# The first norm's transposes: from TensorE to DMA transposes on SP's queue, for three of five groups

## The chip, the cores and the metric

The kernel runs on the 8 cores of one Trainium2 chip, with no communication between them. Cores 0 to 3 take four consecutive quarters (2048 tokens each) of the first sequence, cores 4 to 7 those of the second. The metric is the device time in microseconds of the slowest core.

## The reference

One layer of a diffusion backbone: token mixing (windowed attention with context keys, and a gated spatial MLP per chunk of 128 tokens), then a SwiGLU FFN, each behind a layer norm whose result is scaled and shifted. Cut to the part around the change:

```python
def modulate(y, shift, scale):
    return y * (1 + scale[..., None, :]) + shift[..., None, :]

mod_x = jnp.split(jax.nn.silu(c) @ w_ada[layer] + b_ada[layer], 6, axis=-1)
hc = modulate(layer_norm(ctx), mod_c[0], mod_c[1])     # context tokens
kc, vc = context_kv(hc, w_in[layer])
h = modulate(layer_norm(x), mod_x[0], mod_x[1])        # latent tokens, D_MODEL = 1024
mix = token_mixer(h, *mix_params, kc, vc, (rows, cols))
x_mid = post_norm(x, mod_x[2][:, None, :] * mix, ln1_g[layer], ln1_b[layer])
```

token_mixer multiplies h by w_in: q and k (with rotary positions), v, the two halves u and vb of the gated branch, and two gates.

## The kernel before

The matmuls want the normalised tokens with the 1024 features on the partitions: hT is a bf16 tile of 128 partitions x 8 chunks x 2304 tokens (hcT the same for 256 context tokens). The tokens come in five groups of four 128-token tiles. Groups 0 to 3 are the core's own 2048 tokens; group 4, the outer group, is the tile before, the tile after and the two context tiles. In words of the change's title, group 2 is the third, group 3 the fourth and group 4 the outer one.

For each group:

- x_load (line 289) brings a tile of 128 tokens x 1024 f32, 512 KB, into xin[i], issued from SP.
- ln_stats (lines 413 to 415, VectorE, called DVE in the profile), ln_rstd (lines 418 to 422, GpSimd, called POOL, and DVE).
- ln_norm (line 428, ScalarE, called ACT) writes the normalised tile xnh[i] in bf16 and then has SP issue the x load of the next group into the same xin[i].
- ln_turn (line 442) transposes 128x128 blocks on TensorE (PE) into PSUM banks, a pair of chunks at a time: 8 transposes for 4 tiles.
- ln_out (lines 459 and 463) takes a chunk from PSUM to hT, multiplies by 1 + scale and adds the shift, both per partition (modc, by mcol). Chunks 0, 1, 4 and 5 go by ACT (line 459), 2, 3, 6 and 7 by DVE (line 463).

The projections of a group are units of eight matmuls each: qk_mm (line 488, with the rotary part in qk_rope: one matmul, line 499, two DVE products, lines 503 and 505, one POOL sum, line 511), u_unit (line 528), vb_unit (line 558, followed by a norm of its own in vn_stats and vn_norm, lines 570 to 581) and v_unit (line 540). One do() call emits the units of one group in a written order, and side work behind unit n is taken from a dictionary: side_of(g, at, last) builds it for the norm of the next group. During the units of group g - 1 the positions are: statistics at at + i, norm at at + 4 + i (for the outer group at + i), transposes and evictions from at + 8 on (at + 4 for the outer group). Group 2 has at = 1, groups 3 and 4 have at = 0, and positions over `last` (12; 7 for the outer group) are moved to it.

Other side work in the same stretch: p0_issue loads a block of w_ada (1 MB as bf16, issued from POOL) into one of two buffers, p0_compute multiplies it (lines 349 or 394) and DVE adds the bias (lines 359 or 399). rope_load brings the cosine and sine tables. Each engine runs its queue in the order in which it was emitted. The class Sched puts semaphore waits in front of an instruction for what it depends on.

A transpose by DMA is issued from one queue only, SP's.

Of the kernel before, what the change touches and what calls it, by code (L numbers as in the profile page):

```python
# [9 lines left out]
ALU = mybir.AluOpType  # L10
# [129 lines left out]
def build_nc(debug_stop=None):  # L140
    nc = bass.Bass("TRN2", target_bir_lowering=False)
    es = ExitStack()
    S = Sched()
# [68 lines left out]
    hT, _, nbA = A.alloc(BF16, [8, TH])  # L212
# [36 lines left out]
    def colpos(ti):  # L249
        return {0: 2048, NT + 1: 2176}.get(ti, (ti - 1) * 128)  # L250
# [6 lines left out]
    hcT, _, nb = A.alloc(BF16, [8, CTX], at=o); o += nb  # L257
# [13 lines left out]
    xnh = [A.alloc(BF16, [D], at=at)[0] for at in (  # L271
        RD + 16 * 1024, RD + 18 * 1024, RE_FREE + 20 * 1024, RE_FREE + 22 * 1024)]
# [5 lines left out]
    groups = [[('x', 1 + 4 * g + i) for i in range(4)] for g in range(4)]  # L278
# [46 lines left out]
    def sp_consts():  # L325
        t_gb.append(sp_load(g1bc, badabc_d[:, 0:1024], 'g1b'))
        t_gb.append(sp_load(g2bc, badabc_d[:, 1024:2048], 'g2b'))
        for dst, src in ((bsbc, bsbc_d), (esink, esink_d), (glgc, glgc_d)):
# [7 lines left out]
                 deps=[t_sc])  # L336
# [29 lines left out]
    def mcol(kind, chunk, which):  # L366
        return modc4[:, kind, chunk, which:which + 1]
# [37 lines left out]
    ln = [dict(ag=[None] * 4, xn=[None] * 4) for _ in groups]  # L405
    xnh_free = [None] * 4
    mv_free = [None] * 4
    t_hT = [[None] * 8 for _ in groups]
# [57 lines left out]
            fb_free[banks[n // 2]] = t_hT[g][c] = t_e  # L466


    qraw_free = [None, None]
    rt_free = [None, None]  # L470
    t_qg = [[] for _ in range(4)]
# [123 lines left out]
    t_mod = [[], []]  # L595
# [5 lines left out]
        t_mod[blk % 2].append(t_e)  # L601
    ln_out(0, list(range(8)), [4, 5, 6, 7], t_mod)

    PAIRS = [((0, 1), (3,)), ((2, 3), (6,)), ((4, 5), (7,)), ((6, 7), (3,))]

    def group_seq(g):
        s = []
        if g == 0:
            for n, (kd, m) in enumerate(first):
                s += [(u_unit, m, g)] if kd == 'u' else [(qk_mm, m, g)]  # L610
                if n and first[n - 1][0] == 'q':
                    s += [(qk_rope,)]
            s += [(vb_unit, g, 0), (qk_rope,), (vb_unit, g, 1), (vb_unit, g, 2), (vb_unit, g, 3)]
        else:
            for m in range(4):
                s += [(qk_mm, m, g), (u_unit, m, g), (qk_rope,), (vb_unit, g, m)]
            s += [(qk_mm, 4, g)]
        return s
# [23 lines left out]
    def side_of(g, at, last):  # L642
        side = {}

        def put(n, *work):
            side.setdefault(min(n, last), []).extend(work)

        for i in range(4):
            if g < 4:
                put(at + i, (ln_stats, g, i))  # L650
                put(at + 4 + i, (ln_norm, g, i))
            else:
                put(at + i, (ln_norm, g, i))
            n = at + (8 if g < 4 else 4) + i
            if i:
                put(n, (ln_out, g) + PAIRS[i - 1] + (t_mod,))
            put(n, (ln_turn, g) + PAIRS[i])
        if g < 4:
            side[at + 3].append((ln_rstd, g))
        put(n + 1, (ln_out, g) + PAIRS[3] + (t_mod,))  # L660
        return side

    def bs_sum():
# [8 lines left out]
    def add(side, n, *work):  # L672
        side.setdefault(n, []).extend(work)

    s1 = side_of(2, 1, 12)
    add(s1, 1, (sp_consts,))
    add(s1, 2, (p0_issue,))
    add(s1, 3, (cb_load,))
    add(s1, 6, (p0_compute, 6))
    add(s1, 12, (p0_issue,))  # L680
    s2 = side_of(3, 0, 12)
    add(s2, 1, (p0_compute, 7), (p0_issue,))
    add(s2, 3, (bs_sum,))
# [12 lines left out]


    s3 = side_of(4, 0, 7)
    add(s3, 1, (p0_compute, 1), (p0_issue,))
    add(s3, 7, (p0_compute, 0), (p0_compute, 1))  # L700
# [3 lines left out]
    for k in range(8):  # L704
        t_mm = S.op('pe', lambda e, k=k, pq=bk(b_)[:, 0:CTX]: e.matmul(pq, lhsT=wqk[:, 4, k, :], rhs=hcT[:, k, :],
                                                                     start=(k == 0), stop=(k == 7)),
                    deps=[fb_free[b_], t_hT[4]] if k == 0 else (), sig=(k == 7))
# [420 lines left out]
    for t in range(NT):  # L1128
# [7 lines left out]
        if t % 4 == 3:  # L1136
            g = t // 4
# [21 lines left out]
    for n, (r, tg) in enumerate(order):  # L1159
# [14 lines left out]
        if tg == 3:  # L1174
            if r + NWR < NR:
                load_w1(r + NWR)
            if r == 2:
                for i in range(2, NR):
# [4 lines left out]
                    out=scb2, in_=sc[:, 0:8].unsqueeze(2).to_broadcast([128, 8, 128])), deps=[t_wg2])  # L1183
# [239 lines left out]
```

How the kernel before makes its waits and increments, by code:

```python
            def body(engine, items=items):  # L93
                for (ws, fn, sigkey, inc) in items:
                    for (p, t) in ws:
                        engine.wait_ge(sems[p], t)
                    if fn is None:
                        continue
                    ins = fn(engine)
                    if sigkey is not None:
                        ins.then_inc(sems[sigkey], inc)
```

## Time and profile before

| | |
|---|---|
| median of 3 runs | 987.92 us (987.78 to 989.19) |
| the profiled execution | 987.81 us |
| its span on the slowest core (core 6) | 986.3 us |
| spans of the 8 cores | 978.2 to 986.3 us |
| PE busy | 901.2 us, 91% of the span |
| DVE, ACT, POOL busy | 471.0, 297.2, 243.4 us |
| DMA packets | 41069, 95.50 MB |

The stretch of the trace that the change touches runs from about 84 to 182 us: the units of groups 1, 2, 3 and 4. Times in the rows are microseconds from the start of the span unless marked ns. In a timeline a row is: start, time taken by the row's instructions together, engine, line, operation, and what was idle before it with what ended the wait. A busy PE row ends later than its successor begins, because matmuls are pipelined.

### The profile page before, as it was taken

What the parts mean: (1) busy time and instruction counts of PE and PEld (TensorE: products, weight loads), DVE (VectorE), ACT (ScalarE), POOL (GpSimd) and SP (SyncE); (2) the same over time, 40 slices, a digit from 0 to 9 for tenths busy, and PEclk for the clock granted to TensorE, in tenths of its full rate; (3) what the DMA queues carried; (4) which work ended last, traced back from release to release, by engine and by line L of the source; (5) the groups of instructions that cost most, each with busy time, mean ns of one, the idle gap of its engine ahead of it and who ended that gap; (6) DMA issues with size and microseconds to landing.
All of it is one profiled execution on the core that took longest, in us unless ns stands there. A gap on an engine that the chain in (4) does not pass through costs nothing.

```text
span 986.3 us, 15419 instructions; the slowest of 8 cores (978.2 to 986.3 us)
## 1 busy us (share of the span) xinstructions
PE 901.2 (91%) x5401; PEld 434.9 (44%) x5401; DVE 471.0 (48%) x930; ACT 297.2 (30%) x408; POOL 243.4 (25%) x282
## 2 busy tenths in 40 slices
PE   0569998899999999999989999999999999999993
PEld 0324444445444444444444444444444444444443
DVE  2146665376632456656666321121122114777775
ACT  1215555599922232433333311111111111000000
POOL 5023333256532345555543003010000000000000
PEclk9989999999999999999999999999999999999997
DMA  9988876069720022217713039972211004233231
GB/s 169 169 190 204 175 177 95 3 118 178 137 108 1 1 87 85 73 57 164 157 65 86 22 53 158 167 114 43 35 16 36 1 1 150 92 122 113 101 107 45
DMA packets 41069, 95.50 MB, mean 97 GB/s; under 512 B 4000, under 2 KB 4512, under 8 KB 40992
## 3 DMA queue, kind: packets, MB, share of 16 engines
q0 software_dynamic: 21136, 40.44, 26.6%
q1 hardware_dynamic: 19856, 54.06, 16.9%
q8 instruction: 45, 0.74, 0.3%
q14 instruction: 32, 0.26, 0.1%
HBM read 118.14 MB, written 16.78 MB: 137 GB/s over the span
## 4 chain that ended last, share of the span: by engine, by line
PE 77%; DMA 9%; ACT 5%; DVE 3%; issue 3%; POOL 1%; another core or an unknown queue 0%; SPq 0%; DVEq 0%; ACTq 0%; POOLq 0%
PE bank L1088 30%; PE bank L953 16%; PE bank L1223 14%; DMA arena<-wada 7%; PE bank L984 5%; ACT arena L812 3%; PE bank L488 2%; DMA arena<-xh 2%; PE bank L809 1%; PE bank L558 1%; PE bank L805 1%; PE bank L528 1%; PE bank L828 1%; ACT arena L428 1%; PE bank L1041 1%
## 5 line engine op out<-in xcount | busy, mean ns | idle before, releaser
L1088 PE MATMUL bank<-arena 128*128 128x512 bf16 x1408 | 305.4, 379 | 0.0
L1088 PEld LDWEIGHTS bank<-arena 128*128 128x128 bf16 x1408 | 137.6, 98 | 165.4
L953 PE MATMUL bank<-arena 128*128 128x512 bf16 x768 | 168.0, 379 | 0.0
L1099 DVE TENSOR_TENSOR arena<-bank,arena 128x512 bf16<-128x512 f32 x88 | 60.9, 692 | 224.2 <-PE bank L1088 217.2
L1223 PE MATMUL bank<-arena 128*128 128x512 bf16 (+1 forms) x748 | 152.2, 366 | 0.0
L1097 ACT ACTIVATE arena<-bank 128x512 f32<-128x512 f32 x88 | 52.4, 595 | 224.9 <-PE bank L1088 224.9
L953 PEld LDWEIGHTS bank<-arena 128*128 128x128 bf16 x768 | 75.0, 98 | 89.9
L1223 PEld LDWEIGHTS bank<-arena 128*128 128x128 bf16 x748 | 73.2, 98 | 79.1
L969 DVE TENSOR_TENSOR arena<-bank,arena 128x512 f32<-128x512 f32 x64 | 44.3, 692 | 94.0 <-PE bank L953 94.0
L812 ACT ACTIVATE arena<-bank 128x1024 bf16<-128x1024 f32 x80 | 76.3, 1027 | 4.8 <-PE bank L809 4.5
L962 ACT ACTIVATE arena<-bank 128x512 f32<-128x512 f32 x64 | 37.0, 591 | 118.9 <-PE bank L953 118.9
L971 POOL TENSOR_TENSOR arena<-arena 128x512 bf16<-128x512 f32 x32 | 50.4, 1575 | 71.1 <-DVE arena L969 48.7
L984 PE MATMUL bank<-arena 128*128 128x512 bf16 x256 | 59.0, 384 | 0.0
L1017 ACT ACTIVATE arena<-arena 128x1024 f32<-128x1024 f32 (+1 forms) x32 | 38.5, 1235 | 45.0 <-DVE arena L1015 45.0
L243 POOL DMA_DIRECT2D arena<-wff x22 | 16.4, 763 | 132.9 <-PE bank L1088 132.9
L511 POOL TENSOR_TENSOR arena<-arena 128x512 bf16<-128x512 f32 (+1 forms) x21 | 26.1, 1242 | 86.7 <-DVE arena L505 86.7
L488 PE MATMUL bank<-arena 128*128 128x512 bf16 (+1 forms) x168 | 39.8, 380 | 6.7 <-DMA arena<-wqk 2.6
L1244 ACT ACTIVATE arena<-arena 128x1 f32<-128x1 f32 x16 | 4.7, 294 | 136.3 <-DVE arena L1243 136.3
L1024 POOL TENSOR_TENSOR arena<-arena 128x1024 f32<-128x1024 f32 x16 | 37.7, 2355 | 18.6 <-ACT arena L1017 18.4
L984 PEld LDWEIGHTS bank<-arena 128*128 128x128 bf16 x256 | 25.3, 99 | 30.3 <-issue 1.4
L809 PE MATMUL bank<-arena 64*128 64x512 bf16 x160 | 31.3, 384 | 6.4 <-ACT arena L812 2.7
L558 PE MATMUL bank<-arena 128*128 128x512 bf16 x128 | 33.4, 410 | 3.1 <-DMA arena<-wvvb 3.1
(110 smaller groups left out, 867.2 us busy)
## 6 DMA issues: line engine op xcount, KB each, us to landing
arena<-xh SPq DMA_DIRECT2D x34, 512.0 KB, 6.9
arena<-wada POOLq DMA_DIRECT2D x12, 1024.0 KB, 16.9
arena<-wff POOLq DMA_DIRECT2D x11, 1024.0 KB, 10.4
xmid_d<-arena SPq DMA_DIRECT2D x16, 512.0 KB, 2.9
arena<-xmid_d SPq DMA_DIRECT2D x16, 512.0 KB, 3.7
out<-arena SPq DMA_DIRECT2D x32, 256.0 KB, 2.0
arena<-wff POOLq DMA_DIRECT2D x11, 512.0 KB, 20.6
arena<-wout SPq DMA_DIRECT2D x16, 256.0 KB, 5.4
```

The source lines that it names most:

```text
L488: t_mm = S.op('pe', lambda e, k=k, pq=pq, m=m, rhs=hT[:, k, g * 512:g * 512 + n_]: e.matmul(pq, lhsT=wqk[:, m, k, :], rhs=rhs, start=(k == ...
L558: t_mm = S.op('pe', lambda e, k=k, pvb=bk(b_), lh=hT[:, k, mt * 128:(mt + 1) * 128]: e.matmul(pvb, lhsT=lh, rhs=wvvb[:, k, 128:640], start ...
L809: t_mm = S.op('pe', lambda e, psb=bk(2 * i2 + kv), ksrc=ksrc, kv=kv, j=j, first=not masked: e.matmul(psb, lhsT=ksrc[kv * 64:(kv + 1) * 64, ...
L812: t_e = S.op('act', lambda e, pt=PT[slot], psb=bk2(2 * i2): e.activation(out=pt.rearrange('p a b -> p (a b)'), in_=psb, func=AF.Exp, scale ...
L953: t_mm = S.op('pe', lambda e, k=k, n=n, p=bk(bank), lhs=w[:, lo + k, :], rhs=src[:, k, tok]: e.matmul(p, lhsT=lhs, rhs=rhs, start=(k == 0) ...
L969: fb_free[2 + i] = t_p = S.op('dve', lambda e, dst=sga[r + i], p=bk(2 + i): e.tensor_tensor(out=dst, in0=p, in1=dst, op=ALU.mult), deps=[d ...
L971: t_merged[(m, tg)] = S.op('pool', lambda e, dst=merged[tg % 2][:, m, :], a=sga[r], b=sga[r + 1]: e.tensor_tensor(out=dst, in0=a, in1=b, o ...
L984: rhs=woutb[:, k, half * 512:(half + 1) * 512]: e.matmul(p, lhsT=lhs, rhs=rhs, start=(k == 0), stop=(k == 7)),
L1088: rhs=h2T[:, k, tok]: e.matmul(p, lhsT=lhs, rhs=rhs, start=(k == 0), stop=(k == 7)),
L1097: fb_free[b0] = t_s = S.op('act', lambda e, dst=sgb[s_], p=bk(b0): e.activation(out=dst, in_=p, func=AF.Silu), deps=[t_p[0], sg_free[s_]])
L1099: fb_free[b0 + 1] = sg_free[s_] = t_act[(f, tg)] = S.op('dve', lambda e, f=f, p=bk(b0 + 1), sg=sgb[s_]: e.tensor_tensor(out=act[f][:, tok] ...
L1223: t_mm = S.op('pe', lambda e, pd=bk(b_)[:, 0:cs.stop - cs.start], f=f, t=t, cs=cs: e.matmul(pd, lhsT=act[f][:, t * 128:(t + 1) * 128], rhs ...
```

## The change

For groups 2, 3 and 4 ln_turn and ln_out are replaced by ln_dturn and ln_dmod. ln_dturn(g, i) has SP issue one DMA transpose of a whole tile, xnh[i] (128 tokens x 1024) to the tile's columns in all 8 chunks of hT or hcT. Its completion also frees xnh[i] for the next group. ln_dmod(g, (c, c + 1)) scales and shifts these two chunks in place on DVE once all four transposes of the group are complete; in the outer group each chunk takes two instructions, one for the 256 latent tokens and one for the 256 context tokens. Groups 0 and 1 keep the transposes on PE. The transposes are put right behind the norm of their tile, the ln_dmods at the positions where the evictions stood.

```diff
+    def ln_dturn(g, i):
+        kindt, ti = groups[g][i]
+        dst = hT[:, :, colpos(ti):colpos(ti) + 128] if kindt == 'x' else hcT[:, :, ti * 128:(ti + 1) * 128]
+        xnh_free[i] = ln[g][('dt', i)] = S.dma('sp', lambda e, dst=dst, src=xnh[i]: e.dma_start_transpose(out=dst, in_=src),
+                                               'hturn%d' % i, deps=[ln[g]['xn'][i]])
+
+    def ln_dmod(g, chunks, t_mod):
+        for c in chunks:
+            for h, which in [(hT[:, c, g * 512:(g + 1) * 512], 0)] if g < 4 else [(hT[:, c, 2048:2304], 0), (hcT[:, c, :], 1)]:
+                t_hT[g][c] = S.op('dve', lambda e, h=h, c=c, which=which: e.tensor_scalar(
+                    out=h, in0=h, scalar1=mcol(1, c, which), scalar2=mcol(0, c, which), op0=ALU.mult, op1=ALU.add),
+                    deps=[[ln[g][('dt', i)] for i in range(4)], t_mod[c // 4]])
...
-    PAIRS = [((0, 1), (3,)), ((2, 3), (6,)), ((4, 5), (7,)), ((6, 7), (3,))]
-
...
                 put(at + i, (ln_norm, g, i))
-            n = at + (8 if g < 4 else 4) + i
-            if i:
-                put(n, (ln_out, g) + PAIRS[i - 1] + (t_mod,))
-            put(n, (ln_turn, g) + PAIRS[i])
+            put(at + (4 if g < 4 else 0) + i, (ln_dturn, g, i))
+            put(at + (9 if g < 4 else 5) + i, (ln_dmod, g, (2 * i, 2 * i + 1), t_mod))
         if g < 4:
             side[at + 3].append((ln_rstd, g))
-        put(n + 1, (ln_out, g) + PAIRS[3] + (t_mod,))
         return side
```

## Rows read from the trace of the kernel before

**Rows 1.** The page: busy time, and the chain that ended last.

```profile
PE 901.2 (91%) x5401; PEld 434.9 (44%) x5401; DVE 471.0 (48%) x930; ACT 297.2 (30%) x408; POOL 243.4 (25%) x282
...
PE 77%; DMA 9%; ACT 5%; DVE 3%; issue 3%; POOL 1%; another core or an unknown queue 0%; SPq 0%; DVEq 0%; ACTq 0%; POOLq 0%
```

**Rows 2.** Timeline of PE: the end of group 1's units.

```profile
116.23 0.61 PE L442 MATMUL bank<-arena 128*128 128x128 bf16 x8
116.67 1.95 PE L540 MATMUL bank<-arena 128*128 128x128 bf16 x32
...
118.68 1.89 PE L488 MATMUL bank<-arena 128*128 128x512 bf16 x8
```

**Rows 3.** The chain that ended last, 84 to 190 us: start, length, piece.

```profile
149.59 0.99 DVE arena L463 x2
...
159.40 14.89 DMA arena<-wada
```

**Rows 4.** Timeline of ACT: an eviction pair, the last norm.

```profile
112.42 1.44 ACT L459 ACTIVATE arena<-bank,arena 128x512 bf16<-128x512 bf16 x2
...
163.73 1.23 ACT L428 ACTIVATE arena<-arena 128x1024 bf16<-128x1024 f32 x1
```

**Rows 5.** Line 289 in three short windows: issue times, time to landing.

```profile
L289 SPq DMA_DIRECT2D arena<-xh x1: 328/328/328, 107.8 to 107.8; - x1
...
DMA to landing us min/median/max: 10.8/10.8/10.8
...
L289 SPq DMA_DIRECT2D arena<-xh x1: 327/327/327, 109.8 to 109.8; - x1
...
DMA to landing us min/median/max: 9.9/9.9/9.9
...
L289 SPq DMA_DIRECT2D arena<-ctxb x1: 328/328/328, 139.3 to 139.3; - x1
...
DMA to landing us min/median/max: 5.6/5.6/5.6
```

**Rows 6.** Timeline of DVE.

```profile
111.30 0.68 DVE L503 TENSOR_TENSOR arena<-bank,arena 128x512 f32<-128x512 f32 x1
...
115.39 0.69 DVE L570 BATCH_NORM_STATS2 arena<-arena 128x6 f32<-128x512 f32 x1 [2.10 <-ACT arena L562]
116.19 0.18 DVE L571 BATCH_NORM_AGGREGATE arena<-arena 128x2 f32<-128x6 f32 x1
...
117.58 0.55 DVE L581 TENSOR_SCALAR arena<-arena 128x512 bf16<-128x512 f32 x1 [0.33 <-POOL arena L574]
...
142.48 0.99 DVE L463 TENSOR_SCALAR arena<-bank,arena 128x512 bf16<-128x512 bf16 x2
```

**Rows 7.** Windows: busy us of each engine, granted clock, DMA share, GB/s.

```profile
112.00:116.00 4.00, 4.00 (x29) 2.13 (x27) 1.30 (x2) 2.46 (x4) 1.27 (x1) 1.00 0.98 287
116.00:120.00 4.00, 4.00 (x50) 3.04 (x49) 3.57 (x9) 2.53 (x4) 1.76 (x3) 1.00 0.16 55
...
140.00:144.00 4.00, 4.00 (x32) 2.29 (x31) 2.69 (x7) 2.28 (x4) 1.48 (x3) 1.00 0.91 324
```

**Rows 8.** DMA queues (packets, MB, share), 134.5:145 and then 155:175 us.

```profile
q1 hardware_dynamic: 576, 2.10, 62.2%
q0 software_dynamic: 130, 0.23, 12.2%
...
q0 software_dynamic: 1056, 2.10, 71.0%
q1 hardware_dynamic: 288, 0.26, 6.8%
```

**Rows 9.** Timeline of PE after its longest idle time of the stage.

```profile
156.99 0.99 PE L349 MATMUL bank<-arena 128*128 128x2 bf16 x32 [3.41 <-DVE arena L505]
157.84 2.54 PE L528 MATMUL bank<-arena 128*128 128x512 bf16 x8
160.17 2.97 PE L558 MATMUL bank<-arena 128*128 128x512 bf16 x8
```

## The prediction

> **What bounds it now.** I read the page first. TensorE (PE) is busy for 901.2 of 986.3 us and holds 77% of the chain that ended last, so a microsecond taken from its queue is a microsecond of the span unless something else ends last there [rows 1]. The change touches only the input stage, so I then read PE's timeline there, from 84 to 182 us. It is a string of units of eight matmuls, one every 1.73 us. The eight transposes of a pair of chunks sit between two units and push the next one back by 0.44 us, as from 116.23 to 116.67 [rows 2]. Next I followed the chain that ended last through the same stretch. It leaves PE for long pieces: at 149.59 us it is on the queue of VectorE (DVE), in the scale-and-shift of line 463, and at 159.40 us it is in a load of w_ada that takes 14.89 us; only when that has landed, at 174.3, do PE's matmuls go on [rows 3]. So near the end of this stage DVE's order and the DMA engines set the pace, and PE time saved there is worth nothing.
>
> **What is removed.** 96 transposes leave PE: 12 pairs at 0.44 us, 5.3 us in all. ACT loses its evictions of line 459, 1.44 us a pair of chunks [rows 4]. It waits for PE between most of its operations here, so I value that at nothing.
>
> **What is added to SP's queue, and what stands before it.** ln_norm(g, i) issues the x load of the next group, and ln_dturn(g, i) comes right behind it. SP's order is x(3,0), turn(2,0), x(3,1), turn(2,1) and so on to x(3,3), turn(2,3). A turn waits for the same norm as the load ahead of it, so SP waits no longer than now. But the last transpose is behind a load of 512 KB. In group 2 the last two loads go out at 107.8 and 109.8 us and take 10.8 and 9.9 us, so they land at 118.6 and 119.7, in the order of issue; in group 3 the last goes out at 139.3 and lands 5.6 us later, at 144.9 [rows 5]. If that order holds for transposes as well, the four turns of group 2 are complete no earlier than 119.7 us, however quick they are, and those of group 3 no earlier than 144.9.
>
> Who waits: every ln_dmod depends on all four transposes of its group, and DVE runs its queue in order. DVE meets the first ln_dmod of group 2 just before the rope product that starts at 111.3 us, and that of group 3 at 142.5 us, where a line-463 pair stands now [rows 6]. Behind it on DVE are the rope products, the statistics of the gated branch and the other ln_dmods; PE waits for all of these.
>
> **The price of a transpose** is not in this trace. Each moves 256 KB from SBUF to SBUF. Lower end: at the 324 GB/s seen from 140 to 144 us it costs 0.8 us of all 16 DMA engines [rows 7]. Upper end: each run of 128 columns of one token (256 bytes, 1,024 of them) costs what a small packet costs. From 155 to 175 us 288 packets of the hardware queue, 0.26 MB, took 6.8% of 16 engines for 20 us: 76 ns each, 1.36 us for the quarter megabyte [rows 8]. 1,024 such packets on 16 engines are 4.9 us. I take 2.0 us, near the 1.36 us row and above it, since the pieces are smaller than its packets. Four are 8.0 us per group (3.2 to 19.6).
>
> The Trainium skill, "DMA: Bandwidth & Descriptors", section "Latency and other measured facts", gives 261 GB/s for a DMA transpose with a non-contiguous middle dimension, by estimate 1.0 us each, and with it the sum below would be some 12 us smaller. The Trainium skill, "VectorE: DVE Perf Modes", section "The three transpose paths", speaks against the change: 1309 ns for 128x128 by DMA, 390 ns by TensorE, and TensorE is its advice where the result may go to PSUM. Eight such blocks one after another would by estimate be 10.5 us a transpose and over 100 us in the sum. No row here shows either.
>
> The engines don't stand idle for this. Their share is 0.98 from 112 to 116 us and 0.16 from 116 to 120 [rows 7]: some 2 us are free before 119.7 (part of the rest is the tail of a landing). From 134.5 to 145 us the two queues take 62.2 and 12.2%, so about 2.5 us are free. From 155 to 175 they take 71.0 and 6.8%, of which I give the transposes 2 us [rows 8]. So the landings move back by 6.0, 5.5 and 6.0 us (fast end 1.2, 0.7, 1.2; slow end 17.6, 17.1, 17.6).
>
> **ln_dmod** works on 128x512 bf16 in place in SBUF. Nearest rows: the line-581 normalisation of as many elements, 0.55 us, and the smallest DVE operation beside it, 0.18 us [rows 6]. I take 0.35. Eight are 2.8 us against four evictions at 0.48 (0.96 to 0.99 a pair): +0.9 us per group (-0.5 to +2.5).
>
> **Group 2, step by step.** T is the landing, 119.7 + 6.0 = 125.7. DVE then does two ln_dmods (0.7), two rope products (1.2), statistics and aggregate (0.9), two ln_dmods (0.7): T + 3.5. From the aggregate at 116.19 to the normalisation at 117.58 GpSimd has a step of its own, 1.3 us, so the next normalisation ends at T + 4.6, and the last four ln_dmods at T + 6.0. The first unit of the next group needs the last chunk and so ends at T + 6.2 = 131.9. Now it starts at 118.68 [rows 2] and ends at 120.4. Shift: 11.5 us. The PE time saved in this group lies inside the wait. PE is idle some 10 us in it, and after an idle time of 3.41 us the next two units take 2.54 and 2.97 us in place of 1.89 [rows 9]; I add 1.5 us for that, DVE's backlog hiding the rest.
>
> **Group 3.** In the old times the landing is at 144.9 + 5.5 = 150.4 against DVE's arrival at 142.5. DVE has little idle time from there to 156, and the chain runs through it. Shift: 7.9 + 0.9 = 8.8 us.
>
> **Outer group.** There are no x loads behind its norms, the last of which ends at 165.0 [rows 4]. Its transposes meet the w_ada loads. Its hT is wanted only after the landing at 174.3, so its own landing has 9 us of cover. But that w_ada load is what PE waits for: +6.0 us. The 1.8 us of PE time saved in front of it only lengthen the wait.
>
> Sum: 11.5 + 1.5 + 8.8 + 6.0 = 27.8 us, no PE saving counted. What follows (attention, then FFN) is mostly a closed chain of PE, so it moves as a whole. Against the profiled execution's own 987.8 us (span 986.3 and 1.5 around it; the median of the runs is 987.92, the same to 0.1): 1016 us. Fast end: 6.7 + 1.5 + 4.0 + 1.2 = 13.4, 1001 us. Slow end: 23.1 + 1.5 + 20.4 + 17.6 = 62.6, 1050 us.
>
> **Rivals.**
> (a) The transposes run at plain speed and only the order of the queue costs: 1001 us. For it: they are bytes on the same 16 engines. Against it: 256-byte pieces.
> (b) They are slow: a full packet's cost for each piece, or one after another at what the last 512 KB load took here, 5.6 us [rows 5]. That is the slow end and a little above, 1050 to 1058 us. If a piece costs two packets, one for its reading and one for its writing, it is 9.8 us a transpose, 94 us above my case: 1110 us. The second page of the skill cited above comes out near that.
> (c) The transposes are hidden and the kernel is faster. Mechanism: the order of the queue doesn't bind, so a turn overtakes the load ahead of it. The point is at DVE's arrival: complete by 112 us in group 2 and by 143 in group 3, DVE never waits, and the 8 pairs of these groups save 3.5 us of PE time: 984 us. Against it: that is some 2 and 4 us after the last issue, and the loads in front of them take 9.9 and 5.6.
> (d) Part of the waits remain and the PE time pays for them: no change.
>
> **How the numbers follow.** Chances: my case 0.46 (its own range 1004 to 1032), (a) 0.16, (b) 0.20 up to 1058 and 0.09 beyond, (c) 0.06, (d) 0.03. The likeliest gives 1016. From 996 to 1054 us leaves out (c), (d), the part of (b) near 1110 and a little of the rest. 0.2%, 2 us, is about what a measurement of this kernel can tell from no change: faster 0.06, within it 0.03, slower 0.91.
>
> **What would show it.** Right: 12 transposes on SP's queue; DVE's longest waits are at the new scale-and-shift line, released by a DMA, some 14 us in group 2 and 8 in group 3; PE idle before the first unit that reads hT of group 2 and before the first that reads hT of group 3; the last w_ada load of the stage takes some 20 us to land, not 14.89; from attention on the durations are as before. Wrong: if the turns land within 5 us of issue, the order of the queue was no bound; if a transpose takes more than 3 us of the engines, its price is off and the time is near 1050 us; if the wait in group 3 is absorbed, the chain was not DVE's there.

## The result, and the profile after

The change made the kernel slower. The ratio to the kernel before is 1.0333, with a 95% interval of 1.0296 to 1.0371: 32.9 us more (29 to 37), a time of about 1021 us. The forecast was 1016 us, or 28 us more, in a range from 996 to 1054. All ratios here and below are of executions in which no half of the chip ran at a lower granted clock than the other; of the changed kernel one execution of four (1093.65 us) is left out for that.

The profiled execution (1023.05 us, span 1021.5, slowest core 2) in parts 1, 3 and 4 of the page:

```profile
PE 899.5 (88%) x5228; PEld 431.2 (42%) x5305; DVE 475.4 (47%) x946; ACT 288.3 (28%) x392; POOL 242.8 (24%) x282
...
q0 software_dynamic: 21136, 40.44, 25.4%
q1 hardware_dynamic: 32528, 57.20, 19.5%
...
PE 72%; DMA 7%; DVE 5%; ACT 5%; SPq 4%; issue 4%; POOL 1%; another core or an unknown queue 0%; DVEq 0%; ACTq 0%; POOLq 0%
```

PE is as busy as before [rows 1] in a longer span (77 of its 5305 matmuls, going by the weight loads, are missing from the trace), and the chain that ended last now has 4% on SPq, that is on SP's own instructions. The hardware queue has 12,672 packets more, 1,056 for each of the 12 transposes; by their number and the bytes, that is the 1,024 pieces of 256 bytes and 32 small ones more.

SP's timeline through the input stage: start, time from there to the end of the row's last instruction, line (472 is the transpose, 289 the x load).

```profile
103.25 0.33 SPq L289 DMA_DIRECT2D arena<-xh  x1
103.63 3.20 SPq L472 DMA_TRANSPOSE arena<-arena  x1
106.94 0.51 SPq L289 DMA_DIRECT2D arena<-xh  x1
107.49 5.38 SPq L472 DMA_TRANSPOSE arena<-arena  x1
...
116.33 2.96 SPq L472 DMA_TRANSPOSE arena<-arena  x1
...
145.76 1.32 SPq L472 DMA_TRANSPOSE arena<-arena  x1
...
153.66 1.70 SPq L472 DMA_TRANSPOSE arena<-arena  x1
...
175.21 24.32 SPq L472 DMA_TRANSPOSE arena<-arena  x4
```

This is the part that I had left out. An x load holds SP for 0.33 to 0.53 us; a transpose holds it for 1.3 us at the least and for 5.4 in group 2, and in the outer group four take 24.3 us. In group 2 the second x load goes out 3.7 us behind the first, where it was 1.6 us before, and the next transposes slip with it.

DVE's timeline at the three landings; line 478 is the in-place scale and shift, and the bracket is the wait with what ended it.

```profile
122.70 0.74 DVE L478 TENSOR_SCALAR arena<-arena 128x512 bf16<-128x512 bf16 x2 [11.56 <-DMA arena<-arena]
...
158.99 1.38 DVE L478 TENSOR_SCALAR arena<-arena 128x512 bf16<-128x512 bf16 x4 [5.51 <-DMA arena<-arena]
...
203.36 1.11 DVE L478 TENSOR_SCALAR arena<-arena 128x256 bf16<-128x256 bf16 x4 [16.67 <-DMA arena<-arena]
```

Three waits, 11.6, 5.5 and 16.7 us. The two first were forecast at 14 and 8. The third was not forecast. PE's timeline shows how they arrive at PE:

```profile
124.89 0.58 PE L513 MATMUL bank<-arena 128*128 128x512 bf16 x1 [8.37 <-DVE arena L519]
...
129.85 3.35 PE L542 MATMUL bank<-arena 128*128 128x512 bf16 x8
133.03 1.89 PE L394 MATMUL bank<-arena 128*128 128x512 bf16 x8
...
163.67 2.77 PE L542 MATMUL bank<-arena 128*128 128x512 bf16 x6 [5.10 <-DVE arena L519]
...
174.37 0.99 PE L349 MATMUL bank<-arena 128*128 128x2 bf16 x32 [4.51 <-DVE arena L519]
...
199.14 0.99 PE L349 MATMUL bank<-arena 128*128 128x2 bf16 x32 [9.94 <-DMA arena<-wada]
204.11 0.89 PE L502 MATMUL bank<-arena 128*128 128x256 bf16 x2 [3.97 <-DVE arena L478]
...
216.61 0.39 PE L818 MATMUL bank<-arena 64*128 64x512 bf16 x2 [1.76 <-POOL arena L525]
```

The same instructions in the kernel before:

```profile
122.13 1.89 PE L394 MATMUL bank<-arena 128*128 128x512 bf16 x8
...
174.43 0.99 PE L349 MATMUL bank<-arena 128*128 128x2 bf16 x32 [1.70 <-DMA arena<-wada]
...
182.49 0.39 PE L809 MATMUL bank<-arena 64*128 64x512 bf16 x2 [1.75 <-POOL arena L511]
```

With them the loss can be split by place. The multiplication of a w_ada block that is line 394 in both kernels was at 122.13 us and is at 133.03: 10.9 us for group 2. That of line 349, at 156.99 [rows 9], is at 174.37: 17.4 in all, so 6.5 for group 3. The first score matmul of the attention was at 182.49 and is at 216.61: 34.1 in all, so 16.7 for the outer group. The outer group's part divides once more. The multiplication that waits for the last w_ada load was at 174.43 and is at 199.14, 24.7 us later, so 7.3 of the 16.7 us are the late w_ada load; the other 9.4 us come behind it, from the late transposes, DVE's backlog and the lower clock. From there to the end the shift grows by about 1 us more; the spans of the two profiled executions differ by 35.2.

### The profile page after: what moved, and what is told of

Read it like the earlier page. It is cut to its first block, busy times and chain, and to the rows that moved or that the text cites. A ratio compares the mean times of both kernels' runs of the same rounds, so it can differ in the third digit from the quotient of the medians.

```text
span 1021.5 us, 15196 instructions; the slowest of 8 cores (1011.9 to 1021.5 us)
## 1 busy us (share of the span) xinstructions
PE 899.5 (88%) x5228; PEld 431.2 (42%) x5305; DVE 475.4 (47%) x946; ACT 288.3 (28%) x392; POOL 242.8 (24%) x282
## 4 chain that ended last, share of the span: by engine, by line
PE 72%; DMA 7%; DVE 5%; ACT 5%; SPq 4%; issue 4%; POOL 1%; another core or an unknown queue 0%; DVEq 0%; ACTq 0%; POOLq 0%
PE bank L1097 29%; PE bank L962 16%; PE bank L1232 14%; PE bank L993 5%; SPq L472 4%; DMA arena<-wada 3%; ACT arena L821 3%; DMA arena<-xh 2%; DMA arena<-arena 2%; PE bank L818 1%; PE bank L502 1%; PE bank L837 1%; PE bank L814 1%; DVE arena L478 1%; PE bank L572 1%
## 5 line engine op out<-in xcount | busy, mean ns | idle before, releaser
L1232 PE MATMUL bank<-arena 128*128 128x512 bf16 (+1 forms) x735 | 151.5, 366 | 0.7
L502 PE MATMUL bank<-arena 128*128 128x512 bf16 (+1 forms) x163 | 43.0, 401 | 15.1 <-DVE arena L478 6.9
```

Of the source, the lines that this page charges most:

```text
L502: t_mm = S.op('pe', lambda e, k=k, pq=pq, m=m, rhs=hT[:, k, g * 512:g * 512 + n_]: e.matmul(pq, lhsT=wqk[:, m, k, :], rhs=rhs, start=(k == ...
L1232: t_mm = S.op('pe', lambda e, pd=bk(b_)[:, 0:cs.stop - cs.start], f=f, t=t, cs=cs: e.matmul(pd, lhsT=act[f][:, t * 128:(t + 1) * 128], rhs ...
```

## Experiments

The time differences below are ratio less 1, times 988 us. First, one group at a time.

### The outer group back on PE, and the outer group alone

Without its first line, which lists the chunk pairs of ln_turn again:

```diff
+    DMA_GROUPS = (2, 3)
...
+            if g in DMA_GROUPS:
                 put(at + (4 if g < 4 else 0) + i, (ln_dturn, g, i))
                 put(at + (9 if g < 4 else 5) + i, (ln_dmod, g, (2 * i, 2 * i + 1), t_mod))
+            else:
+                n = at + (8 if g < 4 else 4) + i
+                if i:
+                    put(n, (ln_out, g) + PAIRS[i - 1] + (t_mod,))
+                put(n, (ln_turn, g) + PAIRS[i])
...
+        if g not in DMA_GROUPS:
+            put(n + 1, (ln_out, g) + PAIRS[3] + (t_mod,))
```

In the second kernel DMA_GROUPS is (4,).

Expected of groups 2 and 3 by DMA:

> Groups 2 and 3 by DMA, the outer group back on PE. In the changed kernel's profile the PE units of the outer group's stage came 33 us later than before, of which 17 us were there already at its start. If each group's loss stands by itself, this kernel is 17 to 18 us slower than before: about 1005 us. Rival: the outer group's loss is a follow-up of the earlier shifts (w_ada loads issued later than before meet other traffic), so that they remain here in part: 1010 to 1018 us.

Measured: 1.0176 (1.0149 to 1.0203), 17.4 us.

Expected of the outer group alone by DMA:

> Only the outer group by DMA. If its loss stands by itself: 15 to 16 us slower than before, about 1003 to 1004 us, with the four transposes taking some 20 us of SP's time, as in the changed kernel, next to the two w_ada loads. Rival as for the kernel above: the loss needs the earlier shifts, and alone the outer group costs what I had predicted for it, 6 us: 994 us.

Measured: 1.0136 (1.0118 to 1.0154), 13.4 us. On core 0 the four transposes take 23.0 us of SP's time, about as expected; no other time is read from its trace. So the outer group's loss is its own, not a follow-up of the earlier shifts, and it is twice the 6 us of my prediction.

### Group 2 alone, group 3 alone

The same edit with DMA_GROUPS = (2,) and (3,). Expected of group 2 alone:

> Only group 2 by DMA, in the order of the change. Groups 2 and 3 together cost 17.4 us. If the parts add up, and from the shift of 10 to 11 us behind group 2 in the changed kernel's trace: 10 to 11 us slower than before, about 999 us. Rival: group 3's wait absorbs part of it when both are moved, so group 2 alone costs 12 us or more.

Measured: 1.0104 (1.0085 to 1.0123), 10.3 us. Expected of group 3 alone:

> Only group 3 by DMA, in the order of the change (each transpose behind an x load). With the transposes first it cost 3.6 us. Theory of the queue's order: the last transpose lands 4 to 6 us later for DVE, so 5 to 9 us slower than before, 994 to 997 us. Rival: the order matters only in company with the other groups, 991 to 992 us.

Measured: 1.0102 (1.0083 to 1.0121), 10.1 us, a microsecond over the upper end that I had given. DVE waits 6.72 us for the last transpose here. Groups 2 and 3 together cost 17.4, not 20.4. The wait of group 3 is shorter, 5.51 us, when DVE and PE have been set back by group 2, which may be the reason, but the intervals allow a plain sum too. One by one the three groups make 33.8 us, the whole change 32.9.

### The transposes ahead of the x loads

```diff
+    TURNS_FIRST = (2, 3, 4)
...
-        if g + 1 < len(groups):
+        if g + 1 < len(groups) and g not in TURNS_FIRST:
             x_load(g + 1, i, t_wada0[3])
...
+        if i == 3 and g + 1 < len(groups) and g in TURNS_FIRST:
+            for k in range(4):
+                x_load(g + 1, k, t_wada0[3])
```

The last three lines stand at the end of ln_dturn.

> All three groups by DMA; SP issues a group's four transposes before the four x loads of the next group, not in turn with them. Theory of the queue's order (the last transpose has to wait for the x loads in front of it): the last landing comes 4 to 6 us after the last norm of a group rather than some 13 us in group 2 and 9 in group 3; 4 to 6 us less in each of the two groups, about 1013 us. Rival: the order costs nothing, since SP and the engines move the same bytes either way and the x loads come late for the statistics instead: 1020 to 1025 us.

Measured: 1.0229 (1.0202 to 1.0255), 22.6 us, that is 10.3 us less than the change as made. SP's timeline and DVE's first ln_dmod of groups 2 and 3 (line 474 is the transpose here, 483 the ln_dmod):

```profile
101.39 10.06 SPq L474 DMA_TRANSPOSE arena<-arena  x4
111.50 2.00 SPq L289 DMA_DIRECT2D arena<-xh  x4
...
135.87 6.07 SPq L474 DMA_TRANSPOSE arena<-arena  x4
```

```profile
113.94 0.73 DVE L483 TENSOR_SCALAR arena<-arena 128x512 bf16<-128x512 bf16 x2 [4.91 <-DMA arena<-arena]
...
144.09 1.38 DVE L483 TENSOR_SCALAR arena<-arena 128x512 bf16<-128x512 bf16 x4
```

DVE's wait in group 2 falls from 11.56 to 4.91 us, that in group 3 from 5.51 to none. PE's timeline, at the same places as above:

```profile
123.52 1.89 PE L394 MATMUL bank<-arena 128*128 128x512 bf16 x8
...
160.17 0.99 PE L349 MATMUL bank<-arena 128*128 128x2 bf16 x32 [2.95 <-DVE arena L524]
...
200.21 0.39 PE L823 MATMUL bank<-arena 64*128 64x512 bf16 x2 [1.76 <-POOL arena L530]
```

Against the kernel before that is 1.4 us for group 2 and 1.8 for group 3, where it was 10.9 and 6.5, but still 14.5 for the outer group, which has no x loads on its queue. (The two traces are of different cores, which can differ by a microsecond or so at such a place. Some 4 to 5 us more are lost behind this point; why, no run shows.) The same edit with group 3 alone separates it from the rest:

> Only group 3 by DMA, its four transposes ahead of the x loads on SP. No w_ada load is in flight there, and with all groups by DMA and the transposes first its DVE wait had shrunk to nothing. Theory: what is left is the later x loads (about 3 us) and two microseconds of PE saved in a place where DVE has the chain: 987 to 992 us. Rival: any group by DMA costs several microseconds by itself, through DVE's extra work and the x loads: 993 us or more.

Measured: 1.0036 (1.0023 to 1.0049), 3.6 us, against 10.1 in the old order. The order on SP's queue is worth 6.5 us in group 3 alone. The 3.6 us left go with the x loads: they are issued some 5 us later for the first of them (139.80, where it was 134.48 before), and DVE waits for one:

```profile
142.03 1.38 DVE L483 TENSOR_SCALAR arena<-arena 128x512 bf16<-128x512 bf16 x4 [0.26 <-DMA arena<-arena]
...
146.74 0.69 DVE L413 BATCH_NORM_STATS2 arena<-arena 128x6 f32<-128x512 f32 x1 [3.34 <-DMA arena<-xh]
```

The stall has moved from the transposes to the x loads behind them. This is the fastest of the complete kernels with any group by DMA, and it is still slower than the kernel before.

### The w_ada loads beside the outer group's transposes

Why does SP need 7 to 11 us for one transpose of the outer group? Two w_ada loads are in flight there. The next three kernels leave them out, and multiply the old contents of the two buffers in place of blocks 8 and 9:

```diff
-        t_w = pool_cast_load(flat(wring1[slot]), wada[blk], 'wada_d%d' % slot, deps=[ring1_free[slot]])
+        t_w = None if blk in (8, 9) else pool_cast_load(flat(wring1[slot]), wada[blk], 'wada_d%d' % slot, deps=[ring1_free[slot]])
```

in the changed kernel,

> The changed kernel with the last two w_ada loads of the input stage left out (blocks 8 and 9 are computed with the old contents of their buffers, so the second sub-layer's scale is not the reference's). Theory of contention: a transpose alone costs the DMA engines some 1.4 us (group 3 of the changed kernel), and the 7 to 11 us that SP took to issue two of the outer group's are the work of the software queue's w_ada packets between them. Then all four outer transposes are issued in 1.3 to 3 us each here, land some 5 us after the last norm, and this kernel is 17 to 20 us slower than the kernel before with the same loads left out. Rival: the transposes of the outer group are slow by themselves (another source, another destination, or four in a row without a load between them): SP still takes 5 us or more for each, and the difference to the kernel before without the loads is 25 us or more.

in the kernel before,

> The partner of the kernel above: the kernel before with the last two w_ada loads left out (blocks 8 and 9 computed with the old contents of their buffers). The wait of 1.7 us for w_ada at 174.4 us goes: 985 to 987 us under either theory.

and with the outer group alone by DMA:

> Only the outer group by DMA, and the last two w_ada loads of the stage left out (blocks 8 and 9 computed with the old contents of their buffers). With the loads the outer group alone cost 13.4 us. Theory of contention: without them it costs 0 to 3 us against the kernel before (which was the same with and without the loads): 988 to 991 us. Rival, slow transposes in this group whatever runs beside them: 995 us or more.

Measured against the kernel before: 1.0203 (1.0173 to 1.0232), 0.9994 (0.9973 to 1.0015) and 1.0006 (0.9994 to 1.0017). The loads cost the kernel before nothing that can be told. The changed kernel is 20 us above the kernel before without them, where it was 33, a little over the 17 to 20 us expected. Without them the outer group's transposes cost nothing either, 0.6 us (-0.6 to 1.7), where with them they cost 13.4. The queues and SP's timeline of the changed kernel, with the loads (180 to 188 us) and without (174 to 186 us), then the last kernel: its queue (158 to 170 us) and line 472:

```profile
q1 hardware_dynamic: 853, 0.33, 73.9%
q0 software_dynamic: 234, 0.45, 44.8%
```

```profile
q1 hardware_dynamic: 4512, 1.31, 66.3%
...
174.75 8.36 SPq L472 DMA_TRANSPOSE arena<-arena  x4
```

```profile
q1 hardware_dynamic: 4512, 1.31, 50.9%
...
L472 SPq DMA_TRANSPOSE arena<-arena x4: 1217/1217/1348, 158.5 to 165.9; - x4
...
DMA to landing us min/median/max: 2.8/3.1/3.2
```

With no load beside them the four transposes are complete 2.8 to 3.2 us after issue and hold SP for 1.2 to 1.3 us each (minimum, median and maximum in the last fence, in ns); the 8.36 us of the row above it are mostly SP's waits for the four norms. A packet of the hardware queue (mean of all, the few larger ones of the tables among them) took 0.739 x 16 x 8 us / 853 = 111 ns with the loads. Without them it took 0.663 x 16 x 12 / 4512 = 28 ns in the changed kernel and 0.509 x 16 x 12 / 4512 = 22 ns in the last. While the third transpose is on SP's queue no table is in flight any more; the queues of the changed kernel from 189.8 to 197 us:

```profile
q1 hardware_dynamic: 580, 0.14, 71.1%
q0 software_dynamic: 245, 0.49, 61.3%
```

That is 141 ns a packet. So the pieces were four to six times slower beside w_ada. The two shares add up to more than 100%, so the packets' times overlap and part of them is waiting. But it is a real loss: the two queues together moved 98 GB/s from 180 to 188 us and 88 from 189.8 to 197, less than the 148 GB/s at which the software queue with its w_ada loads went in the kernel before (2.10 MB in 71.0% of 20 us [rows 8]). The second w_ada load, too, took longer to land: 22.6 us, not 14.9.

### The scale and shift at the last position

```diff
-            put(at + (9 if g < 4 else 5) + i, (ln_dmod, g, (2 * i, 2 * i + 1), t_mod))
+            put(last, (ln_dmod, g, (2 * i, 2 * i + 1), t_mod))
```

> The changed kernel with all ln_dmods of a group at the last position of the unit list (12; 7 for the outer group) rather than spread over the last four, so that nothing but the next group stands behind DVE's wait. Theory that DVE's order turns a late landing into a backlog: 3 us less in group 2, 5 in group 3, 1 or 2 in the outer group, about 1014 us. Rival: the landing alone sets the time and DVE would have waited for the same data anyway: 1020 us or more.

Measured: 1.0266 (1.0245 to 1.0286), 26.3 us: 6.6 us less than the change. The time, 1014 us, is as expected, but the gain is less than the 9 to 10 us that its parts were to add up to. The line-349 multiplication behind group 3, where I had expected 8 us, comes only 3.3 us earlier than in the change as made (171.04 against 174.37), though group 3's wait is gone. Group 3 gains 5.6 us, near the 5 expected, but group 2, where I had expected 3 us of gain, loses 2.3: line 394 is at 135.29, where it was at 133.03. Three views, of DVE, of POOL's queue, and of the last transpose of group 2:

```profile
129.80 2.67 DVE L478 TENSOR_SCALAR arena<-arena 128x512 bf16<-128x512 bf16 x8 [13.94 <-DMA arena<-arena]
161.61 2.67 DVE L478 TENSOR_SCALAR arena<-arena 128x512 bf16<-128x512 bf16 x8
```

```profile
115.16 1.02 POOL L243 DMA_DIRECT2D arena<-wada  x1
```

```profile
L472 SPq DMA_TRANSPOSE arena<-arena x1: 2981/2981/2981, 116.3 to 116.3; - x1
...
DMA to landing us min/median/max: 13.2/13.2/13.2
```

In the change as made the stall of DVE also kept POOL waiting, and the next w_ada load went out after the transposes were complete:

```profile
124.78 1.26 POOL L525 TENSOR_TENSOR arena<-arena 128x512 bf16<-128x512 f32 x1 [14.29 <-DVE arena L519]
...
126.94 1.02 POOL L243 DMA_DIRECT2D arena<-wada  x1
```

With DVE free the load goes out at 115.16 and meets them, and the last transpose lands after 13.2 us in place of 6.1. In group 3, where the last w_ada load lands within a microsecond of the first transpose's issue, the wait is gone. The edit on group 3 alone with the transposes first had nothing left to gain:

> As the first of these three (group 3 alone, transposes first), with its ln_dmods at the last position. Theory: with the landing at DVE's arrival there is no wait to move, so this is the same within 2 us of that kernel, 986 to 991 us. Rival: the wait was hidden there too, and moving it gains 3 us or more.

Measured: 1.0041 (1.0028 to 1.0055), 4.1 us, the same as the 3.6 without it.

## Why the prediction was right, and where it was off

**The kind of bound.** Right. No kernel here is faster than the one before, though each takes 32 to 96 transposes from PE; DVE's order and the landings set the pace.

**Order of SP's queue.** Right as the main mechanism in groups 2 and 3: turned round, it gives back 10.3 us of the change and 6.5 of 10.1 us in group 3 alone. The prediction's condition, that a transpose does not overtake the load ahead of it, held: the last x load of group 2 lands at 121.5 us (115.76 + 5.7) and the transpose behind it at 122.4, those of group 3 at 157.7 and 158.7. The floor for the landing was right too: the last transposes land at 122.4 us (116.33 + 6.1) and, less the 10.9 us of shift, at 147.8, against a forecast of 125.7 and 150.4 and floors of 119.7 and 144.9. But "SP waits no longer" missed that the transposes themselves hold SP, so that the x loads behind are late as well. That cost little: the last x load of group 2 went out 6.0 us later than before but landed only 1.8 us later (121.5 against 119.7), since it took 5.7 us in place of 9.9.

**Price of a transpose.** 2.0 us of the engines was high, but not by much, where no w_ada load runs beside it, and far too low beside w_ada. From 145 to 159 us in the changed kernel the hardware queue took 86.5% of the engines; less the 62.2% of 10.5 us for the x loads [rows 8], that is 1.4 us a transpose. Without the w_ada loads the four of the outer group and two small tables took 6.1 us of the engines (50.9% of 12 us), 1.5 a transpose at the most, and in the changed kernel 8.0 us (66.3%), 2.0 at the most. In group 2 four loads of the software queue, the last of which landed at 113.7 us, ran beside the first two transposes, which took 10.9 and 10.7 us to land. Its last landing came at 122.4 us, 3.3 before the forecast 125.7, but DVE's backlog behind it took 1.3 us more than forecast. So group 2 cost 10.9 us and not 13.0, of which 1.5 was the slow clock, as forecast: the first whole unit starts at 129.85 and the next at 133.03, 3.2 us for a unit that took 1.7. The granted clock is 0.50 in the windows from 120 to 132 us, the 1.2 GHz level. Group 3 came to 6.5 us, not 8.8, with the landing 2.6 us before the forecast 150.4.

**ln_dmod.** 0.35 us assumed, 0.33 measured (eight in 2.67 us, in the kernel with the scale and shift at the last position).

**Outer group.** This is the term that was mis-sized: 6.0 us, against 16.7 by the trace and 13.4 alone. The step that failed is the statement that the landing of its transposes "has 9 us of cover" and that they only add their own engine time to w_ada's. I had added up bytes and engine time as if the two queues shared without loss. In fact the w_ada load did come late by about the forecast amount, 7.3 us of shift against 6.0, but the transposes were not covered and added 9.4 us behind it. Their packets became four to six times slower, the second held SP for 10.9 us and the third for 7.1, and the last landed at 203.1 us, 4 us behind the w_ada load that was itself late. Then came the backlog of eight chunks on DVE (to 208.9), while PE's granted clock stayed at its lower level, 0.50, from 192 to 212 us. The forecast of a w_ada landing after 20 us was near: 22.6.

**The rivals.** (a), plain speed, had 0.8 us a transpose; the 1.4 of group 3 lies midway between that and my 2.0, and neither holds for the outer group. (b), slow transposes, was right of the outer group for a reason that I had not given; nothing came near its 1110 us, nor near the estimate from the Trainium skill's 1309 ns a block ("VectorE: DVE Perf Modes", "The three transpose paths"): eight blocks landed together in 3.1 us. The 261 GB/s that the Trainium skill gives in "DMA: Bandwidth & Descriptors" ("Latency and other measured facts") would by estimate be 1.0 us a transpose; the trace has 1.4 in group 3 and far more beside w_ada loads. (c) is out: DVE waited in every group as the change was made. So is (d), no change.

That the total was near is partly luck: groups 2 and 3 were 4.4 us too dear in the forecast, the outer group 10.7 too cheap.

**What stays open.** Whether the packets slow down because the DMA engines take turns between queues, or because a tile of a transpose needs all engines at once, no run here tells apart. Nor does any run put another kind of load than w_ada on another queue beside them. And no placement was found in which the 0.44 us of PE time a pair comes back.

## What to carry to other kernels

A DMA transpose is not a free replacement for PE transposes in a stage where DMA loads are in flight: ask what stands ahead of it in its queue, what runs beside it on other queues, and how long it holds the issuing engine, each with a number from the stage itself. Where one engine waits in order for its landing, the price is landing time plus the backlog behind it, not the bytes. And a stall that is removed may start a load earlier that collides with the very transfer one waits for.

## What the runs showed of the hardware that I had not expected

- A DMA transpose of 128 x 1024 bf16 holds SP's queue: 1.22 us with idle DMA engines, up to 10.9 us (178.8 to 189.7 us in the changed kernel) beside w_ada loads of the software queue; plain loads of 512 KB hold it 0.33 to 0.53 us in the same kernel.
- Alone it is complete 2.8 to 3.2 us after issue; beside two w_ada loads after 21.2, 20.9, 10.9 and 6.1 us.
- It makes 1,056 packets (12,672 for 12). One took 22 and 28 ns in the two kernels without the w_ada loads, 111 to 141 ns beside them.
